# A delta-rule stage in which block products are packed into row halves and corners of the array, decay rows are fetched into two buffers, and a level's product stands ahead of the transposes

## The reference, cut to what matters

```python
def delta_rule_chunked(q, k, v, g, beta, s0):
    ...
    gc = jnp.cumsum(gch, -1)
    decay = jnp.exp(jnp.where(tril, gc[..., :, None] - gc[..., None, :], -jnp.inf))
    kb = kc * bc[..., None]
    vb = vc * bc[..., None]
    m = jnp.where(strict, jnp.einsum('bhncd,bhnsd->bhncs', kb, kc) * decay, 0.0)
    tmat = lax.linalg.triangular_solve(m + eye, jnp.broadcast_to(eye, m.shape), left_side=True,
                                       lower=True, unit_diagonal=True)
    u = jnp.einsum('bhncs,bhnsv->bhncv', tmat, vb)
    w = jnp.einsum('bhncs,bhnsk->bhnck', tmat, kb * jnp.exp(gc)[..., None])
    qk = jnp.einsum('bhncd,bhnsd->bhncs', qc, kc) * decay
    ...
    def step(s, inp):
        u_i, w_i, qk_i, qd_i, kd_i, gl_i = inp
        v_new = u_i - jnp.einsum('bhck,bhkv->bhcv', w_i, s)
        o_i = jnp.einsum('bhck,bhkv->bhcv', qd_i, s) + jnp.einsum('bhcs,bhsv->bhcv', qk_i, v_new)
        s = s * gl_i[..., None, None] + jnp.einsum('bhck,bhcv->bhkv', kd_i, v_new)
        return s, o_i

def gdn_bidirectional(lat, ctx):
    ...
    s_cf, oc_f = delta_rule_chunked(q_c, k_c, v_c, g_c[:, :, 0], b_c[:, :, 0], s0)
    _, ol_f = delta_rule_chunked(q_l, k_l, v_l, g_l[:, :, 0], b_l[:, :, 0], s_cf)
    ...
    return ol_f + fl(ol_b), oc_f + fl(oc_b)
```

## Time and profile before

| | us |
|---|---|
| median of 3 runs | 3584.64 (3584.15 to 3587.2) |
| the profiled execution, time | 3586.9 |
| the profiled execution, span of its instructions | 3585.1 |
| TensorE busy over the span | 3371.8 (94%) |
| mean granted TensorE clock | 0.97 |
| from the first `kk` of the stage to the next stage's first matmul | 1747.9 to 2085.6: 337.7 |
| TensorE busy in it | 300.1 |
| VectorE busy in it | 190.3 |
| GpSimd busy in it | 156.5 |

### The profile page before, as it was taken

The page is one execution under the profiler, slowest core; times in us unless marked ns, Lnnn a source line. Parts: engine busy times, 40 slices in busy tenths (PEclk is TensorE's granted clock), DMA queues, the critical chain, the costliest instruction groups (busy, mean ns, idle before and its releaser), DMA issues.

```text
span 3585.1 us, 40898 instructions
## 1 busy us (share of the span) xinstructions
PE 3371.8 (94%) x16548; PEld 2505.5 (70%) x16548; DVE 1654.0 (46%) x3116; ACT 1228.8 (34%) x2212; POOL 1046.9 (29%) x896
## 2 busy tenths in 40 slices
PE   7999999888899999989799998999999998999998
PEld 3346888655688865645688856888887447848886
DVE  7744446498466666224456524122224117621213
ACT  2413233347323235125433314212213226733222
POOL 0233444450244420011345402222222022024443
PEclk9999999999999999999999999999999999999999
DMA  7424555210355541110111120111111111012222
GB/s 296 186 91 156 206 204 200 88 47 1 111 207 200 200 183 47 47 48 1 32 42 44 28 79 28 71 71 48 71 71 48 53 46 67 1 47 94 97 105 81
DMA packets 67613, 335.42 MB, mean 94 GB/s; under 512 B 32416, under 2 KB 35424, under 8 KB 42592
## 3 DMA queue, kind: packets, MB, share of 16 engines
q1 hardware_dynamic: 66560, 330.56, 25.0%
q10 hardware_dynamic: 864, 2.24, 0.2%
HBM read 325.86 MB, written 6.91 MB: 93 GB/s over the span
## 4 chain that ended last, share of the span: by engine, by line
PE 80%; DVE 10%; ACT 4%; DMA 2%; POOL 2%; issue 2%; SPq 1%; POOLq 0%; DVEq 0%; ACTq 0%
PE PSB L556 17%; PE PSB L648 14%; PE PSB L652 14%; PE PSB L649 14%; PE PSB L1234 3%; PE PSB L1256 2%; PE PSB L1243 2%; PE PSB L2982 1%; DVE SB L389 1%; DMA SB<-in_ada 1%; PE PSB L1795 1%; DVE SB L1328 1%; PE PSB L2419 1%; DVE SB L1639 1%; DVE SB L1637 1%
## 5 line engine op out<-in xcount | busy, mean ns | idle before, releaser
L652 PE MATMUL PSB<-R,WSR 128*128 128x512 f32 x2556 | 871.7, 371 | 0.0
L556 PE MATMUL PSB<-SB 128*128 128x512 f32 x1760 | 655.1, 534 | 11.6 <-ACT SB L1454 9.4
L622 POOL TENSOR_TENSOR WSR<-SB,ahead 128x1024 fp32r<-128x1024 f32 x164 | 393.0, 2397 | 674.1 <-ACT ahead L591 674.1
L556 PEld LDWEIGHTS PSB<-SB 128*128 128x128 f32 x1760 | 338.8, 193 | 325.2 <-issue 298.9
L648 PE MATMUL PSB<-R,ahead 128*128 128x512 f32 x1528 | 561.9, 368 | 0.0
L649 PE MATMUL PSB<-R,ahead 128*128 128x512 f32 x1528 | 546.0, 367 | 0.0
L652 PEld LDWEIGHTS PSB<-R,WSR 128*128 128x128 f32 x2556 | 449.3, 189 | 63.8
L622 POOL TENSOR_TENSOR WSR<-SB,ffn_weights 128x1024 fp32r<-128x1024 f32 x96 | 230.1, 2397 | 390.2 <-ACT ffn_weights L591 390.2
L648 PE MATMUL PSB<-R,ffn_weights 128*128 128x512 f32 x868 | 324.9, 374 | 8.1 <-POOL WSR L622 8.1
L648 PEld LDWEIGHTS PSB<-R,ahead 128*128 128x128 f32 x1528 | 286.9, 188 | 62.9
L649 PEld LDWEIGHTS PSB<-R,ahead 128*128 128x128 f32 x1528 | 286.9, 188 | 48.7
(11 more groups left out here) (377 smaller groups left out, 4888.2 us busy)
## 6 DMA issues: line engine op xcount, KB each, us to landing
SB<-in_w SPq DMA_DIRECT2D x95, 2048.0 KB, 8.1
SB<-in_ada SPq DMA_DIRECT2D x96, 1024.0 KB, 5.1
SB<-gate_rows SPq DMA_DIRECT2D x12, 512.0 KB, 4.4
SB<-in_rpb SPq DMA_DIRECT2D x8, 448.0 KB, 3.5
spill<-SB SPq DMA_DIRECT2D x1, 3072.0 KB, 9.6
SB<-gate_rows SPq DMA_DIRECT2D x24, 128.0 KB, 3.7
SB<-spill SPq DMA_DIRECT2D x1, 3072.0 KB, 9.8
SB<-in_x SPq DMA_DIRECT2D x8, 256.0 KB, 6.3
```

The lines of the kernel that those rows point to most:

```text
L556: ins = e.mm(banks[ring[(g + c) % len(ring)]][0:m, 0:n], t[:, 0:m], xs[k][:, lo:lo + n], k == 0, k == nkt - 1)
L622: e.tt(lr, t, hf, ALU.subtract).then_inc(*G.up(("lo", j)))
L652: ins = e.mm(b[:, 0:n], wl, xh[:, lo:lo + n], False, last)
```

## The change

The products of equal heads are taken in pairs that use different parts of the array. `kk` and `kq` contract over 64 rows each, from the keys directly, for y = 0 and y = 1 in turn (row halves); `KZ`, the copies on ACT and the clearing on POOL go. `md` and `dy` of levels 4 and 5 leave out the zero parts: 16 products of 64 x 64, in turn in the corner of rows and columns 0 to 63 (y = 0) and of 64 to 127 (y = 1), in place of 8 of 128 x 128. DVE's two operations of each step then cover 64 partitions each, with the same 512 elements in each partition. Decay rows have two whole buffers (`DECAY`), the load of chunk n + 2 waits for chunk n only, and stands ahead of the blocks on SP; `decay_arg` moves to the head of DVE's loop. On PE, `md` of level 5 stands ahead of the transposes of level 4, and the first product of level 6 ahead of those of level 5; `kk` and `kq` are no longer split. The diff, cut to its core:

```diff
-            KB, KB1, KZ, DEC = alloc(512), alloc(512), tiles(2, 512), alloc(1024)
+            KB, KB1, DECAY = alloc(512), alloc(512), tiles(2, 1024)
-            Y = tiles(4, 512)
+            Yd = tiles(2, 1024)
+            Y = [Yd[d][:, y * 512:(y + 1) * 512] for d in range(2) for y in range(2)]
-            dec = lambda n: DMd[0] if n == 1 else DEC
-            kb = lambda n: KB1 if n == 1 else KB
+            dec = lambda n: DECAY[n % 2]
+            kb = lambda n: (KB, KB1)[n % 2]
@@ def sp(e):
                 for n in range(12):
-                    if n < 11:
-                        blocks_sp(e, n + 1)
                     if n < 10:
                         gates_in(e, n + 2)
                     if n < 11:
+                        blocks_sp(e, n + 1)
                         inverse_sp(e, n + 1)
@@ def gates_in(e, n):
-                before = 0 if n == 2 else n - 1
                 if n >= 2:
-                    e.wait_ge(*st.at("at", before, 1))
-                    e.wait_ge(*st.at("mt", before, 1))
+                    e.wait_ge(*st.at("at", n - 2, 1))
+                    e.wait_ge(*st.at("mt", n - 2, 1))
                 e.load(dec(n), gate_rows[0, u].partition_broadcast(128)).then_inc(decay_in[d], 16)
                 if n >= 2:
-                    e.wait_ge(*st.at("kk", before, 1))
+                    e.wait_ge(*st.at("kk", n - 2, 1))
@@ kk_pe, and kq in the same way with QT[x][par(y), cl]
-                e.wait_ge(*st.at("key_rows", n, y))
                 for x in range(4):
-                    e.mm(bank(n, "kk", y)[:, col(x)], KZ[y][:, col(x)], kb(n)[:, col(x)]).then_inc(*P.up(("kk", n, y)))
+                    for y in range(2):
+                        e.mm(bank(n, "kk", y)[:, col(x)], KT[x][par(y), cl], kb(n)[par(y), col(x)]).then_inc(*P.up(("kk", n, y)))
@@ pe(e), main loop
-                    for lv in (4, 5):
-                        for y in range(2):
-                            free(e, n, "y", y, lv)
-                            e.wait_ge(*st.at("d", n, y, lv - 1))
-                            for x in range(4):
-                                e.mm(bank(n, "y", y, lv)[:, col(x)], MT[g0 + y][:, col(x)], DM[g0 + y][:, col(x)]).then_inc(*P.up(("md", n, y, lv)))
...
+                    def doubled(lv):
                         for y in range(2):
                             free(e, n, "y", y, lv)
                             e.wait_ge(*st.at("d", n, y, lv - 1))
+                        for h in range(8):
+                            for y in range(2):
+                                e.mm(bank(n, "y", y, lv)[par(y), col(h, 64)], g3(MTd[d])[par(y), h, par(y)], g3(DMd[d])[par(y), h, par(y)]).then_inc(
+                                    *P.up(("md", n, y, lv)))
+                    def corrected(lv):
                         for y in range(2):
                             free(e, n, "d", y, lv)
                             e.wait_ge(*st.at("y", n, y, lv))
                             if lv > 4:
                                 e.wait_ge(*st.at("dt", n, y, lv - 1))
+                        for h in range(8):
+                            for y in range(2):
+                                e.mm(bank(n, "d", y, lv)[par(y), col(h, 64)], g3(DTd[d])[par(y), h, par(y)], g3(Yd[d])[par(y), h, par(y)]).then_inc(
+                                    *P.up(("dy", n, y, lv)))
+                    def turned(lv):
                         for y in range(2):
                             free(e, n, "t", y, lv)
-                            e.wait_ge(*st.at("d", n, y, lv))
+                            e.wait_ge(*st.at("d", n, 1, lv))
                             for x in range(4):
                                 e.tr(bank(n, "t", y, lv)[:, col(x)], DM[g0 + y][:, col(x)], ident).then_inc(*P.up(("dt_T", n, y, lv)))
+                    doubled(4)
+                    corrected(4)
+                    doubled(5)
+                    turned(4)
+                    if n == 11:
+                        out(4)
+                    corrected(5)
                     for y in range(2):
                         free(e, n, "y", y, 6)
-                        e.wait_ge(*st.at("d", n, y, 5))
+                        e.wait_ge(*st.at("d", n, 1, 5))
...
-                    kk(n + 2, 0)
+                    turned(5)
+                    kk(n + 2)
...
-                    kk(n + 2, 1)
...
-                    kq(n + 2, 0)
+                    kq(n + 2)
                     tokens(n + 2, 0)
...
-                    kq(n + 2, 1)
                     tokens(n + 2, 1)
@@ act(e): key_rows_act and its calls go; the copy of y6 stands ahead of the copies of level 5's transposes
+                        if lv == 5:
+                            for y in range(2):
+                                e.wait_ge(*st.at("md", n, y, 6))
+                                e.act(g3(Y[g0 + y])[r, :, q], h3(bank(n, "y", y, 6)[r, 0:256]), ACT.Copy).then_inc(*A.up(("y", n, y, 6), ("read", n, "y", y, 6)))
@@ dve(v), main loop
+                    decay_arg(n + 2)
                     if n >= 2:
...
-                            v.tt(g3(Y[g0 + y]), g3(bank(n, "y", y, lv)), rep(K[("lvF", "lvB")[d]][:, col(lv)]), ALU.mult).then_inc(
-                                *D.up(("y", n, y, lv), ("read", n, "y", y, lv)))
+                            v.tt(g3(Yd[d])[par(y), :, par(y)], h3(bank(n, "y", y, lv)[par(y), :]),
+                                 K[("lvF", "lvB")[d]][par(y), lv * 128 + 64 * y:lv * 128 + 64 * y + 64].unsqueeze(1).broadcast_to([64, 8, 64]),
+                                 ALU.mult).then_inc(*D.up(("y", n, y, lv), ("read", n, "y", y, lv)))
...
-                            v.tt(DM[g0 + y], DM[g0 + y], bank(n, "d", y, lv), ALU.subtract).then_inc(*D.up(("d", n, y, lv), ("read", n, "d", y, lv)))
-                        if lv == 4:
-                            decay_arg(n + 2)
+                            t = g3(DMd[d])[par(y), :, par(y)]
+                            v.tt(t, t, h3(bank(n, "d", y, lv)[par(y), :]), ALU.subtract).then_inc(*D.up(("d", n, y, lv), ("read", n, "d", y, lv)))
```

## The result

The changed kernel took 3700.95 us (median; 3689.32 to 3701.96) against 3585.64, 1.0311 times the time of before (95% interval 1.0298 to 1.0324). I had forecast 3603 and a range up to 3645. It is slower by 115.3 us, six times what I forecast.

A forecast was written before the change was run, and what follows sets the result against it. Two loops at nearly one pace, TensorE with VectorE and SP with GpSimd, were taken to bound it, the former then setting 26.8 us a chunk; chunk changes summed to +18.7 on 3584.64, so 3603 us, range 3590 to 3645.

The forecast's parts named there:

- The sum without the clock: Whole gdn stage with TensorE's clock kept up: chunk changes add 18.7 us to the median, giving 3603.
- levels 4 and 5: Four joint product steps a chunk on TensorE and VectorE: 12.0 us in place of 10.70, +1.3.
- the second and fourth step: Level steps, each a joint product of 1.25, 0.3 of passing and two masks of 1.46: 3.0 us.
- a hand-over of 0.3 us: Passing from a product's last record to VectorE and back to TensorE, 0.3 us in each level step.
- Level 6 to `u`: Level 6's two products, with waits for level 5's copies and VectorE: 4.6 us against 4.23, +0.4.
- `kk` and `kq` as row halves: Eight overlapping row-half matmuls: `kk` 1.0 to 1.1 us, `kq` 0.94 once in place of twice, -0.95.
- Masks on 64 partitions: VectorE's two masks in each level step were assumed to take the same 1.46 us as before.
- TensorE's busy time in the stage: A sign of being right: TensorE's busy time falls by some 50 us, its idle time rises more.
- Loop A: SP and GpSimd's loop of blocks, inverse and return: 25.9 us a chunk, under TensorE's 26.8, so not the bound.
- the return of an inverse: A wait for it ahead of t3 in every chunk would show SP and GpSimd bound; TensorE was forecast to set the pace.
- GpSimd's inverse: A sign on GpSimd: no row of its inverse exceeds 0.4 us, as `decay_arg` ends before it starts.
- the rival that had it fall: TensorE's clock falls once a chunk in the level stage, 2.5 to 3 us each: 3636, up to 3665; chance 0.28.

The follow-up runs named there:

- fill_whole: The changed kernel with 17 unread whole 128x128 matmuls a chunk put into TensorE's waits for VectorE and ScalarE: 3597.26 us, ratio 1.0021.
- order_whole: The changed kernel with level 4 and 5 products and masks whole again, y = 0 before y = 1, the rest kept: 3592.77 us, ratio 1.0012.
- front_parts: The kernel before with only row halves, two decay buffers, gates behind SP's return and `decay_arg` at the chunk's head: 3598.22 us, ratio 1.0024.
- rows_moved: order_whole with gates loaded a chunk earlier in SP's wait for GpSimd and `decay_arg` moved off the chunk's head: 3575.11 us, ratio 0.9972.
- rest_early: rows_moved with GpSimd's subtraction of the past from the values ahead of the inverse, not behind it: 3572.63 us, ratio 0.9960.

## Why the prediction was wrong, point by point

**The sum without the clock was near.** With the clock held, the changed kernel takes 1.0021 times the time of before, 7.5 us, where I had summed 18.7; its stage grows by 11. A chunk takes 26.35 us where I had 26.8. Term by term, from fill_whole's rows: levels 4 and 5 take 11.3 us (1909.95 to 1921.25) where I had 12.0 and before 10.7, because the second and fourth step take 2.70 and 2.61 and not 3.0. The third takes 3.00, as summed, and the first 2.99, for another reason: there the mask waits for `decay_arg`. I had added a hand-over of 0.3 us to a product of 1.25, but the mask begins 1.15 us after the product's start and the next product 0.15 after the mask. Level 6 to `u` takes 4.93 (I had 4.6). `kk` and `kq` as row halves take 1.1 us each for both y, as forecast. Masks on 64 partitions cost what those on 128 cost: that assumption held. TensorE's busy time in the stage, which I had falling by some 50 us, rose from 300.1 to 344.4 in the changed kernel, since so much of the work ran at half clock.

**Loop A.** In the changed kernel TensorE never waits for the return of an inverse after chunk 0, as forecast. In order_whole, whose TensorE needs only 24.8 us a chunk, so that this loop can show its own pace, two turns of SP take 25.9 and 25.3 us (I had 25.9), and TensorE waits twice for an inverse, 1.3 us together. No step of GpSimd's inverse takes over 0.31 us there (0.44 in the changed kernel, for the first of each inverse, beside `decay_arg`, just over my 0.4).

**The step that failed is TensorE's clock: my sum let chunks 1 to 9 keep it at full, a term of nothing, and the rival that had it fall was priced too low.** So its chance (0.28) and the range were wrong too. I named it, with the right place and the right row, as what I least trusted. But I priced it from the 6.4 us that the clock lay at half in chunk 10, as one such stretch in the level stage of each chunk, 2.5 to 3 us, and at most up through `u`: 33 to 62 us. It cost 101.7, and the mean granted clock of the stage was 0.66. Two things were wrong in that. First, I took a length seen once for the length of each fall: here it stayed at half for 34.13 us with TensorE busy for 29.75 of them, all through `kk`, `u`, `kq`, `s`, `o` and `vq`, and half of nearly 30 is 15 us for one fall. The last part of it has no gap at all, and the clock still did not come back:

```profile
2011.83:2027.86 16.03, 16.03 (x91) 0.50 0.06 9
```

Second, I let the evidence for full clock weigh too much: that chunks 1 to 9 ran at 1.00 says little of a kernel that works 1.15 of each 2.70 us. In chunk 6 of before TensorE is busy for 10.22 of the 10.70 us of the two levels; the stretch of before with wider gaps that I had read, 2.71 of 3.40 us, stood right before a fall. The Trainium skill ("TensorE: Matmul & The Clock Gate", the section on a second failure mode) says that frequent short idles between groups of matmuls make the clock oscillate between its levels; the windows of the changed kernel agree, with eight changes in each period of 72 us. The rule has no price in it. An end of the range should have been all of a chunk's work at half clock. In the period shown it is 14.9 us busy at full and 42.9 at half, 36.4 us at full pace or 18.2 a chunk; so a fall that never ends costs up to 18.2 us a chunk, and what was measured, from 26.35 to 35.8 us a chunk, is half of that.

**Not named at all** was that late gates meet `decay_arg` at the chunk's head (2.69 us in front_parts). In the changed kernel, whose chunks are slower, VectorE never waits for those rows from chunk 2 on.

## What to carry to other kernels

Packing small products into tiles pays by the pace of TensorE (1.65 times here) only if TensorE is what is waited for; where another engine must answer each product, keep them whole, as order_whole does (1.0012 against 1.0311), or pack so that two independent groups still alternate, which no run here tried. Before shortening work on an engine with a clock that follows its activity, look in the old trace at the granted clock behind stretches that wait as the new ones will, and price a fall by all the work that lies in a chunk, not by one stretch. Work that nobody reads, put into waits, is a cheap test of whether a loss is the clock, and a second buffer is worth what it lets the queue do behind other work.

## What the runs showed of the hardware that I had not expected

The clock, once down, stayed at half for 34.13 us with 29.75 us of mostly full-width work in it, the last 16.03 us without a gap. With one corner at a time the clock fell in every other chunk, once with TensorE busy for 8.59 of the 10.58 us ahead of it, where two corners in turn with their waits filled kept it for 131.70 us. A third of the added matmuls (6 of 17 a chunk) gave back four fifths of the loss. Small waits matter, but not alone: in chunks 4 to 9 it falls twice in order_whole, which waits 0.70 us for the first mask of each, and not at all in rows_moved, which does not; yet it falls in chunk 1 of rest_early and not in that of rows_moved, with the same waits.
